# Building the first activation tiles: one ScalarE step for the high half, VectorE for the full value, later X scaling, and modulation blocks in new places

## What is computed

```python
cond_p = jax.nn.silu(c_ctx)
cond_s = jax.nn.silu(c)
...
mod_p = jnp.split(cond_p @ ada_w[i] + ada_b[i], 6, axis=-1)
mod_s = jnp.split((cond_s @ ada_w[i] + ada_b[i])[:, None, :], 6, axis=-1)
hp = modulate(xp, mod_p[0], mod_p[1])          # x * (1 + scale) + shift
hs = modulate(xs, mod_s[0], mod_s[1])
...
qp, kp, vp = da_project(hp, da_w_qkv[j])       # h @ w_qkv
qs, ks_, vs = da_project(hs, da_w_qkv[j])
```

## Time and profile before

| | us |
|---|---|
| median of 3 runs | 1747.86 (1747.69 to 1748.56) |
| profiled execution, device time | 1746.07 |
| its span in the profile | 1744.3 |
| PE busy in it | 1690.6 (97%) |
| DVE, ACT, POOL busy | 1090.5, 703.5, 640.9 |
| DMA rate in the first 1/40 of the span (43.6 us) | 362 GB/s, against a mean of 98 |

### The profile page before, as it was taken

How to read it: one execution, slowest core, us unless ns; L and a number is a source line. 1 busy time by engine, 2 the same in 40 slices (tenths; PEclk the granted TensorE clock), 3 DMA queues, 4 the chain that set the end, 5 groups by cost and what they waited for, 6 DMA issues and landing times.

```text
span 1744.3 us, 30097 instructions
## 1 busy us (share of the span) xinstructions
PE 1690.6 (97%) x11440; PEld 1590.4 (91%) x11440; DVE 1090.5 (63%) x1758; ACT 703.5 (40%) x1142; POOL 640.9 (37%) x317
## 2 busy tenths in 40 slices
PE   6999999899999999999999999999999999999996
PEld 4888888598989999899998899998999999999996
DVE  2776777756866515767458664645878861487824
ACT  4455555526332212223237554655463331233324
POOL 4222112356433333323455222124745333333444
PEclk9999999999999999999999999999999999999998
DMA  9312222521444213453221212211212222122221
GB/s 362 132 60 72 67 63 76 212 78 44 183 181 168 89 68 121 168 195 130 84 70 44 75 50 76 76 49 53 87 38 72 74 92 68 69 73 74 84 84 61
DMA packets 59769, 170.97 MB, mean 98 GB/s; under 512 B 7944, under 2 KB 20488, under 8 KB 59664
## 3 DMA queue, kind: packets, MB, share of 16 engines
q1 hardware_dynamic: 51584, 163.33, 27.1%
q10 hardware_dynamic: 8080, 6.18, 1.1%
HBM read 161.07 MB, written 4.74 MB: 95 GB/s over the span
## 4 chain that ended last, share of the span: by engine, by line
PE 73%; DVE 8%; ACT 5%; POOL 4%; issue 4%; DVEq 3%; ACTq 1%; DMA 1%; SPq 0%; POOLq 0%
PE pj L757 59%; POOL wlo L621 3%; PE mO L1242 2%; ACT pr L1596 2%; PE psO L1009 2%; PE pfrow L782 1%; PE psS L974 1%; DVEq L2339 1%; PE st_va L757 1%; POOL ss L635 1%; DVE pr L2353 1%; PE mO L757 1%; PE st_mu L757 1%; PE mS L1198 1%; DVE sm L2338 1%
## 5 line engine op out<-in xcount | busy, mean ns | idle before, releaser
L591 POOL TENSOR_TENSOR wlo<-wraw,whi 128x1024 fp32r<-128x1024 f32 (+1 forms) x118 | 307.8, 2609 | 740.5 <-ACT whi L1384 739.7
L757 PE MATMUL pj<-Hh,whi 128*128 128x320 f32 x2192 | 521.5, 317 | 5.2 <-ACT Hh L1577 4.0
L757 PE MATMUL pj<-Hh,wlo 128*128 128x320 f32 x2192 | 505.3, 309 | 0.0
L757 PE MATMUL pj<-Hl,whi 128*128 128x320 f32 x2192 | 502.3, 309 | 0.0
L757 PEld LDWEIGHTS pj<-Hh,whi 128*128 128x128 f32 x2192 | 365.0, 189 | 29.3 <-issue 20.8
L757 PEld LDWEIGHTS pj<-Hh,wlo 128*128 128x128 f32 x2192 | 368.6, 188 | 0.3
L757 PEld LDWEIGHTS pj<-Hl,whi 128*128 128x128 f32 x2192 | 367.6, 188 | 0.3
L1384 ACT CAST whi<-wraw 128x1024 fp32r<-128x1024 f32 (+1 forms) x168 | 187.5, 1116 | 263.1 <-PE pj L757 227.6
L2246 DVE SCALAR_TENSOR_TENSOR fcv<-fus,vec,fcv 128x127 f32<-128x127 f32 (+1 forms) x176 | 204.3, 1202 | 14.4 <-issue 13.8
L1390 ACT COPY fus<-pj 128x640 f32<-128x640 f32 x84 | 58.3, 696 | 384.3 <-PE pj L757 384.3
L2108 DVE SCALAR_TENSOR_TENSOR X<-pj,mods,X 128x128 f32<-128x128 f32 (+5 forms) x114 | 43.1, 434 | 207.4 <-PE pj L757 207.3
(11 more groups left out here) (371 smaller groups left out, 2408.4 us busy)
## 6 DMA issues: line engine op xcount, KB each, us to landing
wraw<-in_w_up SPq DMA_DIRECT2D x84, 512.0 KB, 3.5
fwr<-in_w_ada SPq DMA_DIRECT2D x56, 512.0 KB, 5.7
wraw<-in_w_dn SPq DMA_DIRECT2D x32, 704.0 KB, 4.0
wraw<-in_w_qkv SPq DMA_DIRECT2D x24, 512.0 KB, 3.5
wraw<-in_w_mlin SPq DMA_DIRECT2D x24, 512.0 KB, 3.4
awr<-in_w_ada SPq DMA_DIRECT2D x16, 512.0 KB, 10.4
awr<-in_w_ada SPq DMA_DIRECT2D x16, 256.0 KB, 7.9
wraw<-in_w_wo SPq DMA_DIRECT2D x8, 512.0 KB, 3.5
```

The costliest lines, as they stand in the source:

```text
L591: nc.gpsimd.tensor_tensor(wlo[k][:, 0:width], wraw[k][:, 0:width], whi[k][:, 0:width].bitcast(F32), ALU.subtract).then_inc(w_lo, 1)
L757: last = mm(out[:, c, 0:HALF], w, x[:, j, c * HALF:(c + 1) * HALF], start=(j == 0 and n == 0), stop=(j == n_k - 1 and n == 2))
```

## The change

Four things change, all ahead of the first head.

1. **High half in one step.** ACT writes `Hh` straight from X (two pieces, no copy), and no longer waits for `h_ready`. The full value `h32` is now made by DVE (`build_full`), which then subtracts; DVE works on two tiles at a time: full, full, low, low.
2. **Coefficients from PSUM.** The biases are put into `la` and `lb` early (`first_bias`); `first_mods` then only adds `pmod` from PSUM to each, in place of one sum into `mods` and two further steps.
3. **X scaling.** POOL multiplies by ALPHA per group of tiles (0 to 3, 4 and 5, 6 and 7), each group when `h_ready` says that all its tiles are done.
4. **PE's order.** Units 0 and 1 take tiles 0 and 1 crosswise; `ada_half(1)` is cut in two: units 8 to 11 ahead of tile 4, units 12 to 15 between the products of tile 5 (unit 0's before, unit 1's behind); `ada_turn(2)` comes ahead of the last products of tile 5; `ada_block(4)` moves behind tiles 0 to 3 of unit 2.

```diff
-            for j in range(KT):
-                pool.wait_ge(h_hi, j + 1)
-                nc.gpsimd.tensor_scalar(X[:, j, :], X[:, j, :], ALPHA, None, ALU.mult).then_inc(x_scaled, 1)
+            for first, end in FIRST:
+                pool.wait_ge(h_ready, end)
+                for j in range(first, end):
+                    nc.gpsimd.tensor_scalar(X[:, j, :], X[:, j, :], ALPHA, None, ALU.mult).then_inc(x_scaled, 1)
...
+            def high_terms(j, ks):
+                pe.wait_ge(h_hi, j + 1)
+                for k in ks:
+                    tile(0, k, [j], pairs=2, read=(), terms=(0, 1))
+            def low_terms(j, ks):
+                pe.wait_ge(h_ready, j + 1)
+                for k in ks:
+                    tile(0, k, [j], pairs=2, terms=(2,))
...
-            first_pair(0, h_ready, 0, 0, js=range(0, 4))
-            ada_half(0)
+            for k in range(2):
+                for j in range(2):
+                    high_terms(j, (k,))
+            for j in range(2):
+                low_terms(j, (0, 1))
+            for j in (2, 3):
+                high_terms(j, (0, 1))
+                low_terms(j, (0, 1))
+            ada_half(0, range(8, 16))
             ada_turn(1)
-            ada_half(1)
+            ada_half(1, range(8, 12))
+            high_terms(4, (0, 1))
+            low_terms(4, (0, 1))
+            high_terms(5, (0,))
+            low_terms(5, (0,))
+            ada_half(1, range(12, 16))
+            high_terms(5, (1,))
             ada_turn(2)
-            first_pair(0, h_ready, 0, 0, js=range(4, KT))
-            ada_block(4)
+            low_terms(5, (1,))
+            for j in (6, 7):
+                high_terms(j, (0, 1))
+                low_terms(j, (0, 1))
             cross(0)
             cross(1)
-            qkv(2, range(0, 7))
+            qkv(2, range(0, 4))
+            ada_block(4)
+            qkv(2, range(4, 7))
             ada_block(5)
...
                 act.wait_ge(xin[j], 16)
-                if j > 1:
-                    act.wait_ge(h_ready, j - 1)
                 for t0, t1, m in SPANS:
-                    fn(h32[j % 2][:, t0:t1], X[:, j, t0:t1], ACT.Identity, scale=la[:, j, m:m + 1], bias=lb[:, j, m:m + 1])
-                act.drain()
-                nc.scalar.copy(Hh[:, j, :], h32[j % 2][:, :]).then_inc(h_hi, 1)
+                    last = fn(Hh[:, j, t0:t1], X[:, j, t0:t1], ACT.Identity, scale=la[:, j, m:m + 1], bias=lb[:, j, m:m + 1])
+                last.then_inc(h_hi, 1)
...
-                tt(m4, pm4, b4[:, :, :, None].to_broadcast([P, 2, n, 2]), ALU.add)
-                dve.drain()
-                ts(la[:, t, :], mod(0, 1)[:, t], 1.0, None, ALU.add)
-                ts(lb[:, t, :], mod(0, 0)[:, t], 1.0, None, ALU.mult).then_inc(coef_ready, 1)
+                tt(la[:, t, :], pm4[:, 1], la[:, t, :], ALU.add)
+                tt(lb[:, t, :], pm4[:, 0], lb[:, t, :], ALU.add).then_inc(coef_ready, 1)
+                dve.drain()
...
+            def build_full(j):
+                dve.wait_ge(xin[j], 16)
+                if j > 1:
+                    dve.wait_ge(h_ready, j - 1)
+                for t0, t1, m in SPANS:
+                    ts(h32[j % 2][:, t0:t1], X[:, j, t0:t1], la[:, j, m:m + 1], lb[:, j, m:m + 1], ALU.mult, ALU.add)
+                dve.drain()
...
-            first_mods(0)
-            for j in range(4):
-                build_lo(j)
-            first_mods(1)
-            build_lo(4)
-            first_mods(2)
-            for j in range(5, KT):
-                build_lo(j)
+            first_bias()
+            for n, (first, end) in enumerate(FIRST):
+                first_mods(n)
+                for j in range(first, end, 2):
+                    build_full(j)
+                    build_full(j + 1)
+                    build_lo(j)
+                    build_lo(j + 1)
```

More of the change, by code:

```diff
@@ L789, in ada_block, with ada_half @@
                 block(n % 2, 2, prow[n // 2 % 2], condp, awr, aw_landed, aw_used, 4 * n)
-            def ada_half(half):
+            def ada_half(half, units):
                 if half:
@@ L795, in ada_half @@
                 c = slice(256 * half, 256 * half + 256)
-                for u in range(8, 16):
+                for u in units:
                     b, kp = u // 4 - 2, u % 4
@@ L2037, in first_mods @@
                 pm4 = pmod[0][:, q, 4 * sd:4 * sd + 4].rearrange("p q (b m) -> p b q m", m=2)
-                m4 = mods[:, 0:2 * KT, :].rearrange("p (b s q) m -> p b s q m", b=2, s=2)[:, :, sd, q]
-                b4 = vec[:, V_ADAB:V_ADAB + 2 * KT].rearrange("p (b s q) -> p b s q", b=2, s=2)[:, :, sd, q]
-                tt(m4, pm4, b4[:, :, :, None].to_broadcast([P, 2, n, 2]), ALU.add)
+                tt(la[:, t, :], pm4[:, 1], la[:, t, :], ALU.add)
+                tt(lb[:, t, :], pm4[:, 0], lb[:, t, :], ALU.add).then_inc(coef_ready, 1)
                 dve.drain()
-                ts(la[:, t, :], mod(0, 1)[:, t], 1.0, None, ALU.add)
-                ts(lb[:, t, :], mod(0, 0)[:, t], 1.0, None, ALU.mult).then_inc(coef_ready, 1)
             def copy_last():
@@ L2060, in pad_cond, with first_bias @@
                 nc.vector.tensor_copy(t[:, :, PAD:PAD + 2], cond[:, :, :]).then_inc(cond_padded, 1)
+            def first_bias():
+                dve.wait_ge(vec_in, 16)
+                b_shift, b_scale = (vec[:, V_ADAB + w * KT:V_ADAB + (w + 1) * KT] for w in range(2))
+                for m in range(2):
+                    ts(la[:, :, m], b_scale, 1.0, None, ALU.add)
+                    ts(lb[:, :, m], b_shift, 1.0, None, ALU.mult)
+            def build_full(j):
[5 more added lines that the diff above has]
+                dve.drain()
             def build_lo(j):
@@ L2312, in _ @@
                 tt(pick[:, :], pick[:, :], ident[:, g:g + 2 * RUN], ALU.add)
-            first_mods(0)
-            for j in range(4):
-                build_lo(j)
-            first_mods(1)
-            build_lo(4)
-            first_mods(2)
-            for j in range(5, KT):
-                build_lo(j)
-            dve.wait_ge(vec_in, 16)
+            first_bias()
[6 more added lines that the diff above has]
+                    build_lo(j + 1)
             lv = vec[:, V_LAM:V_LAM + 4 * DK].rearrange("p (a b) -> p a b", a=4)
```

## The result

The changed kernel takes 1752.89 us in the median of 9 runs (1751.11 to 1754.23), the kernel before 1747.79 in 9 runs beside it (1747.01 to 1750.79). The medians differ by 5.1 us. The ratio is 1.0027, with a 95% interval of 1.0018 to 1.0035: slower by 4.7 us (3.1 to 6.1). The profiled execution took 1751.16 with a span of 1749.3, where before it was 1746.07 and 1744.3.

What follows compares the result with a forecast made beforehand. PE, with 73% of the chain, was taken as the bound, so delaying unit 2 delays the first head. Unit 2 late by 2.1 plus 1.85 for ada_block(4) gave +4.0 on 1747.86: 1751.9 us, range 1748.8 to 1755.8.

Steps and rivals of the forecast that it cites:

- Tiles 0 to 3: Prologue start: PE starts at 20.7, 2.0 us earlier, and finishes these tiles at 31.2, a gain of 1.0.
- The second split behind tile 0: POOL's second split slips in behind tile 0's full value, to 23.25, before tile 1; h_ready 4 at 28.4.
- A scaling stops a new DVE operation to its end: Every build_full waits for POOL's current instruction; tile 4's full value waits 1.6 us for the fourth scaling.
- rival A: POOL doesn't stop the new DVE operations, its queue order stays: H = 43.9, sum +1.5, 1749.4 us; chance 0.18.
- H: Time of h_ready 8, when DVE finishes tile 7's low half: forecast near 45.6 us.
- The wait of units 12 to 15: PE queues them behind tile 5's Hl, so the row copy starts at 40.75 instead of 38.60: loss 2.1 us.
- T = H + 7.1: Start of unit 2 after two scalings, lamp, cast and split: 52.7 against 50.59, late by 2.1 us.
- ada_block(4): Behind tile 3 of unit 2 it no longer fills PE's wait for the split: +1.85 us.
- the row copy: Sign in the profile: the copy for tiles 6 and 7 comes near 40.8, not 38.6.
- a full value of 1.5 us or more for tile 4 or 5: Sign in DVE's profile: a build_full of either tile lasts at least that long.
- an idle PE of over 1 us before unit 2: Sign in the profile: PE idles that long while POOL's split of unit 2 follows the last scaling.
- Rival C: PE's four idle spells make the clock fall again, costing 3.4 us: sum +7.4, 1755.3 us; chance 0.12.

Runs made afterwards that it cites:

- a5: Changed kernel with four extra DVE operations on 640 columns, results unread, while POOL scales tiles 0 to 3; 1753.84 us.
- a3: Changed kernel with units 12 to 15 ahead of tile 4's low products and the turn ahead of tile 5's products for unit 1; 1753.18 us, 1.0021 of before.
- c4: The same kernel as a3, measured again; 1752.12 us, 1.0024 of the kernel before.
- c1: a3's kernel with 12 more matmuls, results unread, in PE's wait between cross and unit 2; 1752.02 us, 1.0024 of the kernel before.
- a1: Changed kernel with ada_block(4) back ahead of the cross matmuls; 1750.95 us, 1.0015 of the kernel before.
- c2: Changed kernel with a2's and a3's edits, so ada_block(4) stays behind tile 3 of unit 2; 1749.15 us, 1.0010 of the kernel before.
- b2: Kernel before with only POOL's scalings in the new groups, each behind the group's last Hl; 1748.92 us, 1.0004 of the kernel before.
- a2: Changed kernel with POOL's splits of units 2 and 3 ahead of the scalings of tiles 6 and 7; 1750.61 us, 1.0012 of the kernel before.
- a4: Changed kernel with the edits of a1, a2 and a3 together; 1748.56 us, 0.9998 of the kernel before.
- c3: Changed kernel unaltered, measured again with a second profile; 1753.15 us (6 runs), 1.0029 of the kernel before.

## Why the prediction was right, and where its terms were not

1751.9 was forecast, slower with a chance of 0.52; 1752.89 came, slower by 0.27%. Against the +4.0 us of its sum stand +3.9 at equal clock and +3.5 in the head. That the path was right is shown by the undoings; that the sum came this near is in part luck, as its terms show. Its steps, each freed of the 0.63 us by which the first row copy was later:

- **Tiles 0 to 3: right.** PE's first `pj` matmul came at 21.33, forecast 20.7 + 0.63. Sums of 0.17 and 0.16 us, ready where they were expected. Tiles 0 to 3 were done at 31.54, or 30.9 without the offset, where 31.2 was forecast and 32.22 was before. This gain was lost again by 41, as the prediction had it.
- **The second split behind tile 0: mis-sized.** It got in between the two instructions of tile 0's full value, not behind them (L2101 in the chain was held for 2.53 us, 21.27 to 23.79). With that, `h_ready` 4 came at 29.6, 0.6 later than the 28.4 + 0.63 forecast.
- **A scaling stops a new DVE operation to its end: failed where it was used.** The rows taken for it were an operation that began 0.75 us into a scaling of 1.42 us (of another form), and a split of 2.88. Tile 4's full value was forecast to wait 1.6 us. It met the fourth scaling at its start, its first piece took 0.82 in place of 0.35, and both tiles took 2.23. Only an operation that begins in a scaling's last part waits for its end. So rival A was half right on this mechanism. It didn't decide, because A also needed H under 45.1 and H was 46.35.
- **H: right in its value, by luck in its terms.** It was forecast at 45.6 + 0.63 = 46.23. Tile 6's full value began at 42.54 where 42.85 + 0.63 was forecast, 0.9 us early. Then the two full values took 2.17 us in place of 1.1, with 0.56 in front of tile 7's that the profile shows as a wait for nothing ("issue"; 0.56 or 0.57 in all profiles with this code except a5, where it is missing). Its cause is open.
- **The wait of units 12 to 15: right.** Row copy at 41.02, forecast 40.75 + 0.63, before 38.60. Undone in a3 and c4, H comes 1.3 us earlier.
- **T = H + 7.1: mis-sized.** It was 6.1. The two scalings took 1.81 to 1.85 us each and not 1.95; why all eight before took 1.91 or more, no run isolates. `lamp` (0.28, before 0.81) and the cast (0.69, from 0.59 us into the second scaling) cost nothing, where 0.25 and 0.55 had been added. For the cast that is luck: PE's products of tile 7, slow at the lower clock, had put it there. In a3, c1, c4 and a5, where PE was earlier, it ran across the boundary of the two scalings, they took 4.02 us, and T - H was 6.5. T came at 52.44, forecast 52.7 + 0.63.
- **`ada_block(4)`: right.** 1.85 us by the chain; its return gave 2.0 in a1, and its move cost 1.56 in c2.
- **Not priced:** 0.46 us in unit 2 itself. Its 42 matmuls took 6.16 us by the chain in one piece right behind `cross`, and 3.79 + 2.83 = 6.62 here. In b2 they took 6.42, in one piece behind a wait for the split. So 0.26 goes with the start behind a wait and 0.20 with taking the unit apart.

With its own numbers the sum for the profiled run is: T 52.44 - 50.59 = 1.85, of which 0.63 is the first row's, plus 1.85 and 0.46: 3.5 in place of 4.0. Terms too large (scaling, cast, `lamp`: -1.1) and too small (0.46, and 0.1 in H) cancelled in part, which is luck. What wasn't luck is the path: a1, a2 and a4 recover 2.0, 1.2 and 4.1 us of the head's shift, and a4 the whole loss; a3's 0.9 shows only in c1, where the clock was kept. Of the signs named beforehand, the row copy, the end of the last scaling and the block in a full stream came; a full value of 1.5 us or more for tile 4 or 5 and an idle PE of over 1 us before unit 2 (0.98) did not.

**Rival C** was given 0.12 as a fall that would cost 3.4 us. The clock did fall again, after the wait of 1.16 us for `Hh` 6: granted 0.50 in 44:47.

```profile
41.00:44.00 3.00, 1.84 (x11) 1.52 (x12) 1.55 (x6) 1.59 (x4) 1.54 (x1) 0.96 1.03 410
44.00:47.00 3.00, 3.00 (x13) 3.00 (x13) 2.82 (x7) 2.04 (x3) 0.57 (x1) 0.50 1.03 410
47.00:50.00 3.00, 2.51 (x14) 2.02 (x14) 0.85 (x2) 1.42 (x3) 3.00 (x2) 0.97 1.01 399
```

It was free here: PE ended tile 7 at 48.98, the cast 49.49, and POOL was busy to 50.03. In c3, a little later, it cost 0.63. The row that I had held against C (1.81 us of idle before 39.07 without a fall) didn't exclude it. The same wait of 1.15 or 1.16 us for `Hh` 6 stands in a1, a2, c3 and a5: a1 lost its clock right behind it, c3 two microseconds later, a2 and a5 kept it. What tells these apart beforehand, the runs don't show.

**What stays open.** The median moved by 5.1 us, the head by 3.5 and 4.2 in the two profiles. At equal granted clock the difference is 3.9, so the head accounts for it. The rest goes with the clock: its mean is 0.9921 over the 15 executions of the changed kernel and 0.9926 over the 88 of the kernel before, which at 1.1 us for each 0.001 is 0.6 us. That difference of clock is about twice its standard error. So it is suggested, and not shown, that the change brings more falls of the clock with it (the one behind `Hh` 6 would be one).

## What to carry to other kernels

Work that an engine did in a gap costs nothing; the same work tied to a later event (here the scalings behind the last subtraction) costs its full length if the next thing in that queue is what another engine waits for. Before moving a block of matmuls, ask whether it was filling a wait: `ada_block(4)` cost 1.6 to 2.0 us for the move alone. And compare starts from a common early event, count the clock's falls in each profile, and compare times at the same granted clock, before a microsecond is called an effect.

## What the runs showed of the hardware

- POOL's `tensor_scalar` in place (128x640, 1.81 us) held up DVE's one-input operations at its two ends and not in its middle: those that began 0 to 0.3 us into it ended as if they had waited to about 0.5 us, those that began at 0.59 and 0.72 ran at full speed, those that began 1.23 us or more into it waited for its end (`la` 0.60 us in place of 0.17, the cast 0.93 in place of 0.69). POOL's `tensor_tensor` of two SBUF tiles held them to its end (2.53 us in the chain), and the next one queued took its place between two DVE instructions.
- DVE delays POOL in turn: a scaling that was due while a DVE operation ran took 2.17 us in a5 (0.49 us operation) and 2.25 in a3 (0.69 us cast), in place of 1.81.
- The granted clock fell for about 3 us at places that are nearly the same in all profiles, but not in each of them. After 2.06 or 2.07 us of idle ahead of unit 2 it fell in three of three profiles, after 0.77 and 0.98 us at the same place it did not; with 12 matmuls in the wait it stayed up. In a3 such a fall made 24 matmuls of 320 columns take 5.24 us in place of 3.79.
- Over 88 executions of one kernel the time went with the mean granted clock: medians of 1746.53 us at 0.994, 1747.80 at 0.993, 1749.23 at 0.992 and 1751.45 at 0.991.
